# A two-block transformer kernel: the mLSTM recurrence on 64-row tiles with its maxima spread by transfers, and attention's preparation and masks moved inside the retention chunks

## The chip, the cores and the metric

One program on one core of a Trainium2 chip. The metric is the device time of one execution in microseconds (us), from the first to the last instruction and what the launch adds around it. Data are float32 throughout. The engines are TensorE (PE, with PEld for its weight loads), VectorE (DVE), ScalarE (ACT), GpSimd (POOL) and SyncE (SP, which here only issues transfers). Each has its own in-order queue of instructions, and semaphores are the only order between them.

## The reference, cut to what matters

The program computes a first block (modulation, four token mixers, a SwiGLU) on a 1024 x 1024 activation with a context of 256 tokens, and then a second block (retention and a sparse attention side by side, an output projection, a gated embedding). Two places are changed. The first is the recurrence of the mLSTM mixer, 4 heads of 64, run in both directions over the tokens:

```
b = cumsum(fc);  logw = where(lower, b[t] - b[s] + ic[s], -inf);  inter = b + m
m_t = max(inter, max(logw));  w_inter = exp(inter - m_t)
s = (qc @ kc.T) * exp(logw - m_t)
num = s @ vc + w_inter * (C @ qc);  den = sum(s) + w_inter * (n @ qc)
h = num / max(abs(den), exp(-m_t))
C = decay * C + e * vc x kc;  n = decay * n + e * kc
```

The second is the pair of retention (8 heads of 64) and sparse attention (8 heads, keys and values from a latent of width 128, each query keeps its 256 best keys):

```
scores = (qc @ kc.T) * intra;  o_intra = scores @ vc;  o_cross = (qc * xi) @ state
state  = chunk_decay * state + (kc * zeta).T @ vc
ret    = head_group_norm(o_intra + o_cross, ret_norm) * silu(r_g)

score  = sum_h wi * relu(qi @ k_idx.T);  top_val, top_idx = top_k(score, 256)
logits = (q_nope @ w_uk) . c_kv[top_idx] + q_pe . k_pe[top_idx]
out    = softmax(logits) @ c_kv[top_idx] @ w_uv
```

## The kernel before

Ten stages follow one another, and each is a block: all engines leave one before they enter the next. Tokens are tiled by P = 128, so the 1024 tokens are NT = 8 tiles and the context NCT = 2. Every stage has one program for each engine, and the order inside an engine's program is the order of its queue.

**stage_mixers** computes the mixers' projections, the short convolution and the gates, and ends with the mLSTM recurrence: 20 steps, 10 tiles in each of 2 directions taken in turn. The first 4 steps (the context) only update the state, the other 16 give output, and the code numbers those `lat` 0 to 15. A direction has four PSUM banks, `4 * d` to `4 * d + 3`. In an output step

- POOL copies the queries into a block-diagonal `qp` (L983), scales the keys into `ke` (L969), and adds the finished output into `H` (L996);
- PE makes the scores of two heads at a time against `qp` (L1109), the products with the carried state `CF` (L1113), the spread of the running maxima over the partitions as products with a selector `sel` (L1096), the state's update (L1126) and the values (L1133);
- DVE adds the keys' column and the mask into `arg` (L1363), ACT takes its exponential (L1203), DVE multiplies it with the scores into `PT` (L1373), scales the carried product into `num` (L1381), updates the state `CS` (L1387), adds the values (L1392), and divides by the bounded denominator (L1395 to L1399).

After the last step the output is normalised by head (L1408 to L1418), transposed, and the next stage starts.

**stage_retention** walks the 8 tiles in order. In tile i, PE makes the scores (L2477) against a block-diagonal `qpad`, transposes the queries and keys of tile i + 1 and attention's queries of it (L2467), makes the update of the state (L2486) from keys that POOL has scaled into `rkz` (L2549), and the output (L2499, L2501) from the state, the weighted scores and a padded copy of the values `vpad`. ACT evicts the transposes (L2512 to L2521) and the output (L2535). DVE multiplies the scores with the decay table (L2591), decays and updates the state (L2596, L2602) and normalises the output of tile i - 1 (`norm`, L2572 to L2580). POOL's order in tile i is: `rkz` (L2549), `xq` (L2554), the gate with the norm's weight (L2555), and the gated product of tile i - 1 (L2559), which waits for that tile's `norm`.

**stage_attention** first prepares: PE transposes the latent (L2671, L2672) and the matrix `uk` (L2675), and makes the values (L2683, 8 products of 512 columns) and the keys (L2691, L2692, 16 products). DVE makes the masks of the tiles 7, 6, 5 and 4 (`mask`, three parts: a count of what lies over the threshold and the flags of what equals it, L2859 to L2861; a running sum of the flags, L2863; the choice, L2865 and L2866), and ACT turns each into 0 or -1e30 (L2788). Then 64 steps (8 tiles of 8 heads, tile 7 first) make logits (L2705), softmax, transposes (L2717) and output (L2730).

**stage_first_end** loads the narrow slab of the second block's input weights in 8 pieces of 2 transfers, each with a semaphore of its own (L1919 to L1921), and splits them on ACT (L1993).

Of the kernel before, what the change touches and what calls it, by code (L numbers as in the profile page):

```python
# [24 lines left out]
P = 128  # L25
# [788 lines left out]
def stage_mixers(K):  # L814
# [38 lines left out]
    mask = K.at("mx_mask", 190.75, [P, 2, P])  # L853
    sel = [K.at(f"mx_sel{d}", kb, [P, HEADS, P]) for d, kb in enumerate((191.75, 6))]

    qp = [K.at(f"mx_qp{d}", 2 + 2 * d, [P, HEADS, P]) for d in range(2)]
# [6 lines left out]
    def columns(n):  # L863
# [22 lines left out]
             "g1 g2 g3 gx gmm ga gb colmm colev st argmm argr pr ptr smm qmm pvmm nr ker umm hr yam yae eps1 eps2 chain pchain").split()  # L886
# [10 lines left out]
    with nc.Block() as block:  # L897
        @block.sync
        def _(sp):
# [18 lines left out]
            load(3)  # L918
            sp.wait_ge(S["pvmm"], 2 * NT)
# [5 lines left out]
        def _(pool):  # L925
# [7 lines left out]
            for t in (selp, mask, *sel, CF, *qp, pair_rows[0]):  # L933
                link(g.memset(t[:], 0.0))
            link(g.memset(d0[:], 1.0))
            for r in (0, 32):
                link(g.affine_select(out=selp[r:r + 4], in_=selp[r:r + 4], compare_op=ALU.not_equal, fill=1.0, base=0,
                                     pattern=[[-2, 2], [-1, 2], [0, HD]], channel_multiplier=1))
                s = sel[r // 32][r:r + 4]
                link(g.affine_select(out=s, in_=s, compare_op=ALU.not_equal, fill=-1.0, base=0,  # L940
                                     pattern=[[-1, HEADS], [0, P]], channel_multiplier=1))
# [3 lines left out]
            link(g.affine_select(out=mask[:, 0, :], in_=mask[:, 0, :], compare_op=ALU.is_ge, fill=LOW, base=0,  # L945
                                 pattern=[[1, P]], channel_multiplier=-1))
            link(g.affine_select(out=mask[:, 1, :], in_=mask[:, 1, :], compare_op=ALU.is_ge, fill=LOW, base=0,
                                 pattern=[[-1, P]], channel_multiplier=1))
# [24 lines left out]
            def queries(n):  # L973
                step, d = steps[n]
                lat = n - 2 * NCT
                if lat < 0:
                    return
                if lat >= 2:
                    pool.wait_ge(S["qmm"], lat - 1)
                tok = slice((order[d][step] - NCT) * P, (order[d][step] - NCT + 1) * P)  # L980
                for a in range(2):
                    hr = slice(a * HD, (a + 1) * HD)
                    g.tensor_copy(qp[d][hr, a::2, :], qkT[hr, 0:2, tok]).then_inc(S["qp"], 1)  # L983
                pool.wait_ge(S["qp"], 2 * (lat + 1))
# [3 lines left out]
            for n, (step, d) in enumerate(steps):  # L988
                lat = n - 2 * NCT
                if n + 2 < len(steps):  # L990
                    queries(n + 2)
                    keys(n + 2)
                if lat >= 0:
                    c = order[d][step] - NCT
                    pool.wait_ge(S["xr"], lat + 1)
                    g.tensor_tensor(H[:, c], H[:, c], num[d][:, :, 0:HD], ALU.add).then_inc(S["hadd"], 1)  # L996
                    pool.wait_ge(S["hadd"], lat + 1)

        @block.tensor
        def _(pe):  # L1000
# [88 lines left out]
            def argument(n):  # L1089
                step, d = steps[n]  # L1090
                c = order[d][step]
                if c < NCT:
                    return
                pe.wait_ge(S["st"], n - 1)
                for h in range(HEADS):
                    last = nc.tensor.matmul(K.bank[4 * d][:, h * P:(h + 1) * P], sel[d][:, h, :], lrows[:, c * P:(c + 1) * P], start=True, stop=True)  # L1096
                last.then_inc(S["argmm"], 1)

            for n, (step, d) in enumerate(steps):
                c, lat = order[d][step], n - 2 * NCT  # L1100
                b = [K.bank[4 * d + m] for m in range(4)]
                tok = slice((c - NCT) * P, (c - NCT + 1) * P)
                if lat >= 0:
                    if lat >= 2:
                        pe.wait_ge(S["nr"], lat - 1)
                    pe.wait_ge(S["st"], n - 1)
                    pe.wait_ge(S["qp"], 2 * (lat + 1))
                    for j in range(2):
                        last = nc.tensor.matmul(b[1].rearrange("p (h t) -> p h t", h=HEADS)[:, 2 * j:2 * j + 2, :], qkT[:, 2 + j, tok],  # L1109
                                                qp[d][:, 2 * j:2 * j + 2, :], start=True, stop=True)  # L1110
                    last.then_inc(S["smm"], 1)
                    for h in range(HEADS):
                        last = nc.tensor.matmul(b[2][:, h * P:(h + 1) * P], qp[d][:, h, :], CF[:, d, h // 2 * HX:h // 2 * HX + P],  # L1113
                                                start=True, stop=True)
                    last.then_inc(S["qmm"], 1)
                if n + 1 < len(steps):
                    argument(n + 1)
                if step < NL - 1:
                    pe.wait_ge(S["ker"], n + 1)
                    if lat >= 0:  # L1120
                        pe.wait_ge(S["argr"], lat + 1)
                    elif n >= 2:
                        pe.wait_ge(S["st"], n - 1)
                    for h in range(HEADS):
                        o = (h // 2) * HX
                        last = nc.tensor.matmul(b[0][(h % 2) * HD:(h % 2 + 1) * HD, o:o + HX], ke[d][:, h, :], vx[:, c, h, :],  # L1126
                                                start=True, stop=True)
                    last.then_inc(S["umm"], 1)
                if lat >= 0:
                    pe.wait_ge(S["ptr"], lat + 1)  # L1130
                    for h in range(HEADS):
                        o = (c * HEADS + h) * HX
                        last = nc.tensor.matmul(b[3][:, h * P:(h + 1) * P], PT[d][:, h, :], vflat[:, o:o + P], start=True, stop=True)  # L1133
                    last.then_inc(S["pvmm"], 1)
# [8 lines left out]
        def _(act):  # L1143
# [54 lines left out]
            for q in range(4):  # L1198
                act.wait_ge(S["yb_tr"], q + 1)
                nc.scalar.activation(K.yT[2 + q // 2][:, (q % 2) * HALF:(q % 2 + 1) * HALF], K.bank[q][:], ACT.Copy).then_inc(S["yb_ev"], 1)  # L1200
            for m in range(2 * NT):
                act.wait_ge(S["argr"], m + 1)
                nc.scalar.activation(arg[m % 2][:], arg[m % 2][:], ACT.Exp).then_inc(S["pr"], 1)  # L1203
# [18 lines left out]
        def _(dve):  # L1222
# [118 lines left out]
            link(v.tensor_tensor(chunked(lf), chunked(lf), before, ALU.max))  # L1341
            link(v.tensor_tensor(chunked(win), before, chunked(lf), ALU.subtract))
# [13 lines left out]
            def argument(n):  # L1356
                step, d = steps[n]
                c = order[d][step]
                if c < NCT:
                    return  # L1360
                dve.wait_ge(S["argmm"], n - 2 * NCT + 1)
                for h in range(HEADS):
                    last = v.scalar_tensor_tensor(out=arg[d][:, h, :], in0=K.bank[4 * d][:, h * P:(h + 1) * P], scalar=COL[:, 1, c, 1, d, h:h + 1],  # L1363
                                                  in1=mask[:, d, :], op0=ALU.add, op1=ALU.min)
                last.then_inc(S["argr"], 1)

            for n, (step, d) in enumerate(steps):
                c, lat = order[d][step], n - 2 * NCT
                b = [K.bank[4 * d + m] for m in range(4)]
                if lat >= 0:  # L1370
                    dve.wait_ge(S["pr"], lat + 1)
                    dve.wait_ge(S["smm"], lat + 1)
                    v.scalar_tensor_tensor(out=PT[d][:], in0=b[1].rearrange("p (h t) -> p h t", h=HEADS), scalar=HD ** -0.5, in1=arg[d][:],  # L1373
                                           op0=ALU.mult, op1=ALU.mult).then_inc(S["ptr"], 1)
                if n + 1 < len(steps):
                    argument(n + 1)
                if lat >= 0:
                    if lat >= 2:
                        dve.wait_ge(S["hadd"], lat - 1)
                    dve.wait_ge(S["qmm"], lat + 1)  # L1380
                    link(v.tensor_tensor(num[d][:], b[2].rearrange("p (h e) -> p h e", h=HEADS)[:, :, 0:HX],  # L1381
                                         COL[:, 0, c, 0, d, :].unsqueeze(2).to_broadcast([P, HEADS, HX]), ALU.mult))
                if step < NL - 1:
                    dve.wait_ge(S["umm"], n + 1)
                    for j in range(2):
                        o = j * HX
                        last = v.scalar_tensor_tensor(out=CS[:, d, j, :], in0=CS[:, d, j, :], scalar=dcol[:, d, j, c:c + 1],  # L1387
                                                      in1=b[0][:, o:o + HX], op0=ALU.mult, op1=ALU.add)
                    last.then_inc(S["st"], 1)
                if lat >= 0:  # L1390
# [1746 lines left out]
```

## Time and profile before

| | |
|---|---|
| time, median of 3 runs | 2272.81 us (2270.8 to 2273.53) |
| the profiled execution: its time, its span | 2270.93 us, 2269.1 us |
| PE busy in the span | 2117.0 us (93%) |
| DVE busy | 1278.9 us (56%) |
| ACT busy | 733.0 us (32%) |
| POOL busy | 435.1 us (19%) |
| mean granted TensorE clock | 0.963 |

A row of a timeline gives the start and the duration in us from the start of the span, the engine, the line of the kernel, the operation, what it writes and reads, the number of instructions merged into the row, and in brackets the engine's idle time ahead of it and what ended that. The busy share of an engine is an average over stages with different limits, so what a change in one stage is worth is read in that stage. A float32 product is two MATMUL instructions, a transpose one.

### The profile page before, as it was taken

The page shows a single profiled execution, that of the slowest core. Times are in us where ns is not written, and L with a number is a line of the kernel's source. Part 1 is how long each engine was busy: PE and PEld are TensorE (multiplying, and loading weights), DVE is VectorE, ACT ScalarE, POOL GpSimd, SP SyncE. Part 2 cuts the span into 40 slices and gives each one's busy share as a digit, 9 for nine tenths or more (in the row PEclk, how much of TensorE's full clock was granted, in tenths as well). Part 3 has the DMA queues.
Part 4 walks back from the last instruction along what each step waited for, and adds up shares of the span by engine and source line. Part 5 has one row for each costly group of instructions (what it writes and reads, how often), then busy time and mean ns, then how long its engine had stood idle before and what let it go on. Part 6 is the DMA issues. An engine that isn't in the chain of part 4 may idle for free. (4 is left out here: it accounts for less than half of the span.)

```text
span 2269.1 us, 27732 instructions
## 1 busy us (share of the span) xinstructions
PE 2117.0 (93%) x10549; PEld 1599.9 (71%) x10549; DVE 1278.9 (56%) x2211; ACT 733.0 (32%) x1292; POOL 435.1 (19%) x501
## 2 busy tenths in 40 slices
PE   7998999995969999999999998889999868989998
PEld 4744464484858888888888886856888764658876
DVE  6591895278864333223454324478999577762433
ACT  2222021122113323223444223356121335761415
POOL 2900011042310000000000001223666440300210
PEclk8999999997989999999999999899999889999999
DMA  8543110003233333334434232122211002003101
GB/s 325 155 134 116 42 46 1 0 2 121 75 102 93 93 97 89 90 106 147 121 111 130 81 97 87 58 56 61 66 47 50 20 3 81 2 25 130 51 0 75
DMA packets 187512, 180.59 MB, mean 80 GB/s; under 512 B 12982, under 2 KB 157686, under 8 KB 184074
## 3 DMA queue, kind: packets, MB, share of 16 engines
q1 hardware_dynamic: 184426, 168.61, 23.9%
q0 software_dynamic: 2880, 10.49, 1.2%
q8 instruction: 70, 1.15, 0.2%
q14 instruction: 40, 0.33, 0.0%
q10 hardware_dynamic: 96, 0.02, 0.0%
HBM read 165.18 MB, written 12.60 MB: 78 GB/s over the span
## 5 line engine op out<-in xcount | busy, mean ns | idle before, releaser
L1800 DVE TENSOR_TENSOR ff_part<-ff_raw,ff_part 128x1024 fp32r<-128x1024 f32 (+2 forms) x152 | 164.9, 1085 | 435.5 <-ACT ff_part L1708 435.5
L1708 ACT ACTIVATE ff_part<-ff_raw 128x1024 fp32r<-128x1024 f32 (+2 forms) x152 | 144.0, 948 | 433.4 <-PE ps L1598 430.9
L1596 PE MATMUL ps<-h,ff_part 128*128 128x512 f32 x704 | 275.5, 391 | 4.7 <-DVE ff_part L1800 4.7
L1598 PE MATMUL ps<-h,ff_part 128*128 128x512 f32 x704 | 274.7, 390 | 0.0
L1597 PE MATMUL ps<-h,ff_part 128*128 128x512 f32 x704 | 274.7, 390 | 0.0
L2416 DVE TENSOR_SCALAR_CACHE_REDUCE pj_junk<-NM,prm 128x384 uint8<-128x384 f32 (+1 forms) x186 | 163.7, 942 | 1.1
L1596 PEld LDWEIGHTS ps<-h,ff_part 128*128 128x128 f32 x704 | 132.8, 189 | 32.3 <-DVE ff_part L1800 5.1
L1596 PE MATMUL ps<-pj_part,h 128*128 128x512 f32 x384 | 153.2, 399 | 0.2 <-ACT PJ L2273 0.2
L1597 PEld LDWEIGHTS ps<-h,ff_part 128*128 128x128 f32 x704 | 132.8, 189 | 27.4
L1598 PEld LDWEIGHTS ps<-h,ff_part 128*128 128x128 f32 x704 | 132.6, 188 | 27.6
L1597 PE MATMUL ps<-pj_part,h 128*128 128x512 f32 x384 | 150.4, 392 | 0.0
L1598 PE MATMUL ps<-pj_part,h 128*128 128x512 f32 x384 | 150.2, 391 | 0.0
L1597 PE MATMUL ps<-ff_hid,ff_part 128*128 128x512 f32 x352 | 137.0, 389 | 0.0
L1598 PE MATMUL ps<-ff_hid,ff_part 128*128 128x512 f32 x352 | 137.0, 389 | 0.0
L1596 PE MATMUL ps<-ff_hid,ff_part 128*128 128x512 f32 x352 | 137.0, 389 | 0.0
L2358 POOL TENSOR_TENSOR pj_part<-pj_raw,pj_part 128x512 fp32r<-128x512 f32 x64 | 84.7, 1326 | 160.3 <-ACT pj_part L2268 159.0
L1596 PE MATMUL ps<-w_end,se_hT 128*128 128x512 f32 x256 | 106.9, 418 | 0.4 <-DVE se_hT L3066 0.4
L1003 PE MATMUL ps<-mx_w,HT 128*128 128x272 f32 (+1 forms) x320 | 106.2, 493 | 0.0
L1598 PE MATMUL ps<-w_end,se_hT 128*128 128x512 f32 x256 | 100.0, 390 | 0.0
L1597 PE MATMUL ps<-w_end,se_hT 128*128 128x512 f32 x256 | 99.7, 390 | 0.0
L1596 PEld LDWEIGHTS ps<-pj_part,h 128*128 128x128 f32 x384 | 72.5, 189 | 29.4 <-issue 14.4
L1003 PEld LDWEIGHTS ps<-mx_w,HT 128*128 128x128 f32 x320 | 60.7, 190 | 44.2 <-issue 38.0
(601 smaller groups left out, 4057.7 us busy)
## 6 DMA issues: line engine op xcount, KB each, us to landing
ff_raw<-in_w_ffn_in SPq DMA_DIRECT2D x88, 512.0 KB, 3.7
s_wm<-in_w_mod SPq DMA_DIRECT2D x16, 1024.0 KB, 4.9
pj_raw<-in_w_in SPq DMA_DIRECT2D x64, 256.0 KB, 2.7
ff_raw<-in_w_ffn_out SPq DMA_DIRECT2D x32, 384.0 KB, 3.4
ff_raw<-in_w_ffn_out SPq DMA_DIRECT2D x32, 320.0 KB, 3.0
mod_w<-in_w_mod SPq DMA_DIRECT2D x8, 1024.0 KB, 8.9
mod_x<-in_x SPq DMA_DIRECT2D x8, 512.0 KB, 13.9
w_out<-in_w_out SPq DMA_DIRECT2D x4, 1024.0 KB, 8.7
```

What stands on the lines that cost most here:

```text
L1003: mm = nc.tensor.matmul(bank[:, 0:cols], lhs, rhs, start=(k == 0), stop=(k == KT - 1))
L1596: nc.tensor.matmul(out, w[0], x[0], start=first, stop=False)
L1597: nc.tensor.matmul(out, w[0], x[1], start=False, stop=False)
L1598: return nc.tensor.matmul(out, w[1], x[0], start=False, stop=last)
L1708: nc.scalar.activation(part[s % 2][0][:, 0:n, :], raw[s][:, 0:n, :], ACT.Copy).then_inc(hi, 1)
L1800: v.tensor_tensor(part[s % 2][1][:, 0:n, :], raw[s][:, 0:n, :], part[s % 2][0][:, 0:n, :].bitcast(F32), ALU.subtract).then_inc(lo, 1)
L2358: g.tensor_tensor(part[k % NR][1][:], raw[k % NR][:], part[k % NR][0][:].bitcast(F32), ALU.subtract).then_inc(S["lo"], 1)
L2416: last = v.tensor_scalar(junk[:, packed(j + 2)], x, bound(j), 0.0, ALU.is_ge, ALU.add, accum_out=cnt[:, j:j + 1])
```

## The change

Mixers, recurrence:

- The block-diagonal `qp` and POOL's two copies for it go. Scores and carried products read `qkT` directly, a head's 64 rows at a time, even heads into one bank and odd heads into another (`place` gives the order of heads in `arg` and `PT`).
- The products with `sel` go, and so do `sel`, `mask` and their preparation. Once DVE has the running maxima, they are written to DRAM, and SP reads them back for each step into a ring of 8 tiles `spread` of 128 x 512, each row repeated over all partitions (16 transfers of 256 KB in pieces of 512 bytes). POOL hides the future with an affine select on the tile (`hide`), 4 steps ahead.
- ACT takes the exponential straight from the ring, a head at a time with the keys' column as bias (`weights`), and scales the carried product (`carried`), also a head at a time. DVE's `argument` and the first product into `num` go, and its closing work of a step is done a step later (`finish`). POOL's addition into `H` is a step later too.
- The values' product takes 65 columns in place of 128.

Retention and attention:

- `qpad`, `vpad` and ACT's copies for them go: scores and output work on 64 rows or 64 columns a head. The scaled keys are written over the keys. The state's decay is done by ACT, a head pair at a time. Attention's queries are transposed ahead of the chunks.
- The transposes of the latent, attention's keys and values, the matrix `uk` and its transfers leave stage_attention. The latent is transposed at the start of the retention and evicted by DVE; in each chunk PE makes one tile of the values and one half row of the keys in bank 2, and ACT evicts both.
- The mask of tile 7 is made by DVE ahead of the chunks, one part of the masks 6, 5 and 4 in each chunk after `norm`, the last one at the end; ACT lowers them in chunks 1, 4 and 7 and at the end.
- SP loads the tables `intra` and `xi` and the norm's row only after attention's queries have been transposed.

First end: the 8 pieces of the narrow slab share 4 semaphores.

The core of the diff:

```diff
+            sp.wait_ge(S["lfr"], 1)
+            for d in range(2):
+                sp.dma_start(lf_dram[d], lf[32 * d:32 * d + HEADS, :]).then_inc(lf_out, 16)
+            sp.wait_ge(lf_out, 32)
+            sp.wait_ge(S["mm"], total)
+            for m in range(2 * NT):
+                step, d = steps[2 * NCT + m]
+                c = order[d][step]
+                if m >= RING:
+                    sp.wait_ge(S["pr"], m - RING + 1)
+                sp.dma_start(spread[m % RING][:], lf_dram[d:d + 1, :, c * P:(c + 1) * P].to_broadcast([P, HEADS, P])).then_inc(lf_in[m % RING], 16)
...
             for n, (step, d) in enumerate(steps):
                 lat = n - 2 * NCT
                 if n + 2 < len(steps):
-                    queries(n + 2)
                     keys(n + 2)
+                if n == 0:
+                    for m in range(4):
+                        hide(m)
                 if lat >= 0:
-                    c = order[d][step] - NCT
-                    pool.wait_ge(S["xr"], lat + 1)
-                    g.tensor_tensor(H[:, c], H[:, c], num[d][:, :, 0:HD], ALU.add).then_inc(S["hadd"], 1)
+                    hide(lat + 4)
+                if lat >= 1:
+                    gather(lat - 1)
...
+                for j in range(2):
+                    for a in range(2):
+                        r = slice(HD * a, HD * (a + 1))
+                        nc.tensor.matmul(b[a][:, j * P:(j + 1) * P], qkT[r, 2 + j, tok], qkT[r, j, tok], start=True, stop=True)
+                for j in range(2):
+                    for a in range(2):
+                        r = slice(HD * a, HD * (a + 1))
+                        last = nc.tensor.matmul(b[a][:, 2 * P + j * HX:2 * P + (j + 1) * HX], qkT[r, j, tok], CS[r, d, j, :], start=True, stop=True)
...
+            for n in range(len(steps)):
+                update(n)
                 if n + 1 < len(steps):
-                    argument(n + 1)
+                    scores(n + 1)
+                values(n)
...
+                for h in range(HEADS):
+                    last = nc.scalar.activation(arg[d][:, place(h), :], spread[m % RING][:, h, :], ACT.Exp, scale=-1.0, bias=COL[:, 1, c, 1, d, h:h + 1])
+                for h in range(HEADS):
+                    o = 2 * P + h // 2 * HX
+                    last = nc.scalar.activation(num[d][:, h, :], K.bank[4 * d + 1 + h % 2][:, o:o + HX], ACT.Copy, scale=COL[:, 0, c, 0, d, h:h + 1])
...
+            for i in range(NT):
+                turn_queries(i)
+                turn_latent(i)
...
+                prepare(2 * i)
+                if i + 1 < NT:
                     pe.wait_ge(S["kzr"], i + 1)
...
+                prepare(2 * i + 1)
                 pe.wait_ge(S["prob"], i + 1)
...
+            for part in range(3):
+                mask(FIRST[0], part)
             dve.wait_ge(S["const"], 80)
...
                 if i + 1 < NT:
                     new = state[1 - s]
                     if i:
-                        link(v.tensor_tensor(new[:], state[s][:], decay.unsqueeze(2).to_broadcast([P, J, P]), ALU.mult))
+                        dve.wait_ge(S["dec"], i)
                     dve.wait_ge(S["upd"], i + 1)
...
                 if i:
                     norm(i - 1)
+                mask(FIRST[1 + i // 3], i % 3)
             norm(NT - 1)
+            mask(FIRST[3], 2)
```

## Rows read from the trace of the kernel before

**Rows 1.** Windows by engine: length, then busy us (instructions) of PE, PEld, DVE, ACT, POOL; clock.

```profile
464.40:531.20 66.80, 63.48 (x548) 58.77 (x546) 59.15 (x201) 9.45 (x15) 29.24 (x56) 1.00 0.03 6
...
1782.70:1867.70 85.00, 61.90 (x400) 56.71 (x400) 53.34 (x100) 33.91 (x73) 43.71 (x37) 0.86 0.04 13
1867.70:1899.90 32.20, 27.60 (x68) 13.78 (x68) 23.96 (x30) 13.41 (x34) 0.66 (x2) 0.85 0.41 145
```

**Rows 2.** Timeline of one output step of the recurrence.

```profile
489.83 1.06 PE L1096 MATMUL ps<-mx_lf,mx_sel 128*128 128x128 f32 x8
...
490.32 0.68 POOL L996 TENSOR_TENSOR mx_H<-mx_H,mx_num 128x256 f32<-128x256 f32 x1 [1.84 <-DVE mx_num L1399]
...
490.81 0.45 PE L1126 MATMUL ps<-mx_vx,mx_ke 128*64 128x65 f32 x8
490.92 1.12 DVE L1363 SCALAR_TENSOR_TENSOR mx_arg<-ps,mx_COL,mx_mask 128x128 f32<-128x128 f32 x4
...
491.19 1.16 PE L1133 MATMUL ps<-mx_vx,mx_PT 128*128 128x128 f32 x8
...
491.99 0.61 POOL L969 TENSOR_TENSOR mx_ke<-mx_kn,mx_COL 128x256 f32<-128x256 f32 x1
...
492.41 0.47 DVE L1387 SCALAR_TENSOR_TENSOR mx_CS<-mx_CS,prm,ps 128x65 f32<-128x65 f32 x2
492.81 0.42 DVE L1392 TENSOR_TENSOR mx_num<-mx_num,ps 128x260 f32<-128x260 f32 x1
...
493.95 1.06 PE L1096 MATMUL ps<-mx_lf,mx_sel 128*128 128x128 f32 x8
494.22 0.68 DVE L1373 SCALAR_TENSOR_TENSOR mx_PT<-ps,mx_arg 128x512 f32<-128x512 f32 x1
```

**Rows 3.** Timeline of retention's start: POOL's keys alone, the first weighted scores.

```profile
1791.86 1.04 POOL L2549 TENSOR_TENSOR rt_kz<-PJ,prm 128x512 f32<-128x512 f32 x1
...
1792.48 1.29 DVE L2591 TENSOR_TENSOR rt_prob<-ps,rt_intra 128x512 f32<-128x512 f32 x2 [14.76 <-PE ps L2477]
```

**Rows 4.** Timeline of retention: one round of POOL, PE and DVE.

```profile
1815.94 1.29 POOL L2559 TENSOR_TENSOR PJ<-PJ 128x512 f32<-128x512 f32 x1 [4.88 <-DVE PJ L2580]
...
1824.70 0.69 DVE L2580 TENSOR_TENSOR PJ<-PJ,prm 128x512 f32<-128x512 f32 x1
...
1826.77 1.49 POOL L2549 TENSOR_TENSOR rt_kz<-PJ,prm 128x512 f32<-128x512 f32 x1
...
1829.58 0.85 DVE L2602 TENSOR_TENSOR rt_state<-rt_state,ps 64x256 f32<-64x256 f32 x2 [2.22 <-PE ps L2486]
```

**Rows 5.** Timeline of attention's logits, 64-row tiles: start of eight and of what follows.

```profile
1911.70 1.99 PE L2705 MATMUL ps<-at_kT,dqT 64*128 64x512 f32 x8
1913.61 1.09 PE L2717 MATMUL ps<-ident,at_prob 128*128 128x128 f32 x8
```

**Rows 6.** Groups of ACT: the eviction of 128 x 128.

```profile
L2761 ACT ACTIVATE at_latT<-ps 128x128 f32<-128x128 f32 x8 | 2.3, 283 | 3.4 <-PE ps L2672 3.4
```

**Rows 7.** One line of POOL: an affine select over 512 columns.

```profile
L940 POOL TENSOR_SCALAR_AFFINE_SELECT mx_sel<-mx_sel x2: 625/626/626, 329.9 to 331.3; 4x512 f32<-4x512 f32 x2
```

**Rows 8.** Transfers by tile: KB, median us from issue to landing.

```profile
at_wuv<-in_w_uv SPq DMA_DIRECT2D x1, 256.0 KB, 2.9
```

**Rows 9.** Timeline of retention's last chunk: POOL and DVE at once.

```profile
1856.16 1.27 POOL L2555 TENSOR_TENSOR PJ<-PJ,rt_row 128x512 f32<-128x512 f32 x1
1856.26 1.71 DVE L2574 TENSOR_TENSOR PJ<-PJ,prm 128x512 f32<-128x512 f32 x1
```

**Rows 10.** Timeline of attention's preparation: DVE's masks of the tiles 7 and 6.

```profile
1868.14 1.26 DVE L2859 TENSOR_SCALAR_CACHE_REDUCE at_flag<-NM,prm 128x1024 uint8<-128x1024 f32 x1
...
1875.39 1.15 DVE L2859 TENSOR_SCALAR_CACHE_REDUCE at_flag<-NM,prm 128x896 uint8<-128x896 f32 x1
...
1877.49 2.02 DVE L2863 TENSOR_TENSOR_SCAN at_run<-at_flag 128x896 f32<-128x896 uint8 x1
...
1881.92 1.01 DVE L2859 TENSOR_SCALAR_CACHE_REDUCE at_flag<-NM,prm 128x768 uint8<-128x768 f32 x1
```

More of the change, by code:

```diff
@@ L932, in _ @@
             link = Link(g, S["pchain"])
[L933 removed]
+            for t in (selp, CF, pair_rows[0]):
                 link(g.memset(t[:], 0.0))
@@ L1087, in _, with scores @@
             pe.wait_ge(S["yb_ev"], 4)
[L1089 removed]
+            def scores(n):
                 step, d = steps[n]
[L1091 to L1092 removed]
+                c, lat = order[d][step], n - 2 * NCT
+                if lat < 0:
                     return
[L1094 to L1097 removed]
@@ new lines, in values @@
+            def values(n):
+                step, d = steps[n]
+                c, lat = order[d][step], n - 2 * NCT
+                if lat < 0:
+                    return
+                pe.wait_ge(S["ptr"], lat + 1)
+                if lat >= 2:
+                    pe.wait_ge(S["nr"], lat - 1)
+                for h in range(HEADS):
+                    last = nc.tensor.matmul(K.bank[4 * d + 3][:, h * P:h * P + HX], PT[d][:, place(h), :], vx[:, c, h, :], start=True, stop=True)
+                last.then_inc(S["pvmm"], 1)
@@ L2445, in stage_retention @@
     mu, var = (K.prm[:, 16 + RH * n:16 + RH * (n + 1)] for n in range(2))
-    names = "zero vr const tr qkr dqr smm prob xqr kzr out oev upd state var gate norm done chain".split()
+    K.kfT = K.at("at_kT", 24, [P, J, T])
+    K.val = K.at("at_v", 40, [P, NT, AH * AD])
+    lat_pe = K.at("at_latpe", 80, [P, 2, T])
+    latT, peT = lat_pe[:, 0], lat_pe[:, 1]
+    ukT = K.at("at_ukT", SMALL_KB, [P, J, P])
+    wuv = K.at("at_wuv", SMALL_KB + 2, [P, AH, AD])
+    spread = K.at("at_spread", SMALL_KB + 4, [P, 2, AD])
+    uk = K.wsT
+    names = ("zero const tr qkr dqt dqr smm prob xqr kzr out oev upd state var gate norm done chain "
+             "clear uk wuv spread dec turn latr ukr pre prer pick masked").split()
     S = {n: K.sem("rt_" + n) for n in names}
@@ L2531, in _ @@
                     take(i + 1)
+                prepared(2 * i)
+                if 0 < i < NT - 1:
+                    act.wait_ge(S["state"], i)
+                    for j in range(J):
+                        last = nc.scalar.activation(state[1 - i % 2][:, j, :], state[i % 2][:, j, :], ACT.Copy, scale=decay[:, j:j + 1])
+                    last.then_inc(S["dec"], 1)
+                prepared(2 * i + 1)
                 if i:
```

435 lines of the change are left out of this document (217 added, 218 removed).

## The prediction

> **What bounds the kernel now.** I read the page's slices first, then the windows of the stages that the diff touches, then the timeline inside one period of each, since both are loops. Three stretches matter [rows 1]. In the recurrence's output part PE (63.5 of 66.8 us) and DVE (59.2) are both nearly full. In the retention (85.0 us) no engine is: PE 61.9, DVE 53.3, POOL 43.7, ACT 33.9. Attention's preparation takes 32.2 us, with PE busy for 27.6, and POOL does almost nothing there.
>
> One step of the recurrence repeats every 4.12 us, from L1096 to the next L1096 [rows 2]. PE issues 36 instructions in it without a pause: eight of L1096 take 0.98 us to issue (0.12 each), eight of L1126 with 65 columns 0.38 (0.048), L1133 goes like L1096. The reader is to see that DVE's programme is as long: it goes from the argument at 490.92 to the next PT at 494.22 with gaps of some 0.03 only.
>
> In the retention a ring of waits sets the pace, not an engine. POOL's L2559 starts at 1815.94 and the next of its kind about 9.6 us later: `norm` ends at 1825.39 (1824.70 + 0.69), POOL multiplies by the gate (1.29), scales the keys (1.49, from 1826.77), PE makes the update (1.2), DVE adds it to the state at 1829.58, and then comes the next `norm`, which ends about 5.4 later [rows 4]. So from the end of `norm` to the state's addition pass 4.19 us, in which DVE has only the scores and the decay to do.
>
> The preparation is a sequence ahead of the first logits and ends where PE's products end.
>
> **The recurrence, part by part.** DVE: the argument and the carried product go, which is 490.92 to 492.41, 1.49 us. Left are 4.12 - 1.49 = 2.63 us [rows 2]. PE: L1096's 0.98 goes. The scores become eight instructions of 128 columns on alternating halves of the rows. The nearest rows are attention's logits, already in such halves: eight of 512 columns in 1.91 us, 0.24 each [rows 5], about half of four times 0.12. So I take 0.06 each, 0.5 us; the upper end is 0.12, 1.0 us. Carried product, update and values are eight instructions of 65 columns each: 0.38 us by L1126, up to 1.0 by L1133, if 128 columns of weights set the pace. PE needs 1.7 to 3.4 us (0.5 to 1.0, 0.4, and twice 0.4 to 1.0); I take 2.4. ACT: eight pieces of at most 0.28 [rows 6], 2.3 us instead of 0.63. POOL: the copies go, an affine select of 0.63 comes [rows 7]; with 0.68 for H and 0.61 for the keys [rows 2] and gaps it has 2.2 us. The transfers: the nearest is 256 KB in pieces of half the size, which landed after 2.9 us [rows 8]; eight are under way ahead of use, so 2.9 a step would still be hidden. The cover gone, a step would be as long as a transfer.
>
> No engine alone needs more than 2.6. But POOL and DVE get in each other's way: in the last chunk DVE's product takes 1.71 us behind a POOL product that ends 1.2 us after it began, where the same kind takes 0.69 [rows 9, 4]. In the new step POOL's three operations run from DVE's last product on, 2.25 us. DVE meanwhile does PT, the states and the first addition (0.68 + 0.40 + 0.45 = 1.55, with PSUM as an input), then comes to the small products and the scaling, 494.22 - 493.26 = 0.96 us (the addition at 492.81 takes 0.45 with its gap) [rows 2], all from SBUF. If those must wait for POOL's third operation, the step is 2.25 + 0.96 = 3.2. With a little for handshakes I take 3.25. Bounds: 2.63 without exclusion; 3.6 if PE needs its upper end with changes of tile shape between.
>
> Between the first and last PT lie 15 steps: 15 x (4.12 - 3.25) = 13.0 us gained. At the head POOL makes four selects (2.6 us) between the keys of steps 2 and 3; the context's updates wait, but the first PT waited for the argument before. I charge 0.5. The first ring tiles are read once the last slab's products are done, some 6 us before use, so they are hidden. The tail has the same chain. Recurrence: -12.5 us (bounds -22 and -7). Everything behind it moves up.
>
> **Retention and preparation.** Gone: 32.2 us of preparation [rows 1]. Added, at three places:
>
> Front. Before, the first weighted scores came at 1792.48 [rows 3], 9.8 us into the stage. Now 60 transposes at 0.12 us, the first 13 or so at twice that (8 to 9 us), and DVE's eight evictions stand first, until about 1791. Then comes the mask of tile 7, 7.25 us (1868.14 to 1875.39) [rows 10], and POOL's first two products (1.04 [rows 3] and 1.3, released by the late tables near 1795.5) fall between its parts. First weighted scores near 1800.6, +8.1; about +7.5 is left at the first `norm`'s end, as chunk 0 was waiting for other things too.
>
> Chunks. Each gets a mask part between `norm` and the scores. For tile 6 these are 2.10, 2.06 and 2.37 us (1875.39 to 1877.49; the scan with its gap; the rest up to 1881.92) [rows 10]; the scores take 1.29 [rows 3]. By length alone, at most 2.37 + 1.29 = 3.7 fits into the 4.19, and the ring would stay near 9.3 (the decay has left DVE, and POOL's keys, 1.49 beside it [rows 4], take 1.04 alone [rows 3]). But the part's operations start 0.1 us ahead of POOL's gated product. With exclusion: count part, the flags wait for the keys, state at 4.6; scan 2.0 + 1.29 + 1.04 + 1.2 = 5.6; choice, two passes with a POOL product between them, 5.8. Over 4.19 that is 0.4, 1.4 and 1.6. No row shows a scan beside POOL; it has two inputs from SBUF like the row that waited [rows 9], so I take the full wait, and nothing as the lower end. Five rounds carry a part (scan, choice, count, scan, choice, the last three shorter): +6.1 us.
>
> The Trainium skill (SBUF — State Buffer, "SBUF: two separate sides") has it that VectorE with two SBUF inputs and a GpSimd operation share one port pair under an exclusive lock, and the loser blocks for the whole instruction. The product that waited agrees (1.71 for 0.69) [rows 9]; for scan and choice no row here shows it. By that rule the chunks cost the 6.1 above, without it they would gain about 1.
>
> PE has some 7.8 us a chunk now (scores 1.0, transposes 1.0, three products of 512 columns and two passes 2.6, update 1.0, output 2.2), below the ring. ACT has 4.1 us and in three chunks 0.9 more. Their place in the queue matters: the second product of the preparation stands between update and output, 1.7 us, which the output can bear as long as it is evicted before the `norm` of the next round.
>
> Tail. The last mask's three parts (tile 4, some 5.0 us by columns, from 6.5 for tile 6) fall into the last two chunks and behind, with 0.7 for ACT to lower it; I guess that 1.3 of it hides in the wait for the last output. +4.4.
>
> Sum: 7.5 + 6.1 + 4.4 = 18.0 us added, 32.2 gone: -14.2. Without exclusion front and chunks lose 2.4 and 7.0 of that: -23. If PE or ACT hold up `norm` in each round by 1.3 us, -7. The first end's paired semaphores: a piece waits for the second pair's transfers, issued 0.9 us later, while PE has transposes to do; nothing.
>
> **Sum.** 2270.9 (the profiled execution) - 12.5 - 14.2 = 2244.2. The median of the runs, 2272.8, is 1.9 above that execution, so on its scale 2246.
>
> **Rivals.**
> - Exclusion costs little, since the queues fall into step so that POOL and DVE rarely meet, as they now do in the recurrence. For it: POOL is idle for half of both loops. Against: the new order starts both at the same event. Step 2.63, ring 9.3: -22 - 23 = -45, 2228.
> - Chunks and steps are longer: PE without the pairing's gain (step 3.6) and a queue in the chunks that holds `norm` up: -7 - 7 = -14, 2259.
> - The spreading by transfers doesn't do what it should: a read of 512-byte pieces takes a whole old step (4.1 us) once eight are queued. The recurrence gains nothing, 2259. Against it stands 2.9 [rows 8].
> - Slower than before: the clock. Granted were 0.86 in the retention with PE busy 73% of the time, 1.00 in the recurrence at 95% [rows 1]. Afterwards PE is busy for about 74% in both (2.4 of 3.25, 7.8 of 10.7). If it is granted the lower level throughout (1.2 GHz), a step takes 4.8 us (+10), and eight chunks of 15.6 and a front of 15 make 140 us against 117 now (+23): 2306. It decides from a mean near 0.6 in both on, below which a step (2.4 / 0.6 = 4.0) and a chunk (13) are as long as what they save. The 0.86 at the same share of busy time speaks against it.
>
> **Chances.** Forecast 0.56, exclusion costs little 0.18, longer steps and chunks 0.16, transfers 0.05, clock 0.05. The first has its own range of 2236 to 2257 (the uncertain sizes in step and ring). To leave out no more than 2 in 10 it must reach the neighbours on both sides, 2230 to 2262. Under 0.2% (4.5 us) this kernel can't tell a change. All but the clock are far on the fast side; a milder clock gives about 0.03 for no change: faster 0.92, same 0.03, slower 0.05.
>
> **What the next profile would show.** Right: PTs 3.2 to 3.3 us apart, DVE's first small product starting as POOL's third operation ends; the retention 103 us long, with rounds near 11.0, and DVE's scans followed at once by POOL's gated product; first logits about 0.4 us into attention. Wrong: PTs 2.6 apart or rounds near 9.3 with the scan beside a POOL product; ACT or PE busy up to each `norm`; a recurrence whose wait is for `spread`; a granted clock under 0.7.

## The result, and the profile after

The changed kernel takes 2258.25 us (median of 4 runs, 2257.96 to 2262.19) against 2272.96 for the kernel before: ratio 0.9945, 95% interval 0.9933 to 0.9958. That is 14.7 us faster, where 26.8 were forecast. The profiled execution takes 2257.96 us, its span is 2256.2 against 2269.1, and its mean granted clock 0.951 against 0.963.

Put side by side by stretches, the two executions differ so (us; "readout" is the first reduction of the recurrence's output; a norm counts to its last product's end):

| stretch | before | after | change | forecast |
|---|---|---|---|---|
| start to first PT | 464.45 | 464.85 | +0.4 | +0.5 |
| first to last PT | 62.35 | 63.96 | +1.6 | -13.0 |
| last PT to readout | 4.36 | 5.88 | +1.5 | 0 |
| readout to the retention's first instruction | 1251.54 | 1247.72 | -3.8 | 0 |
| to the first norm's end | 23.04 | 32.90 | +9.9 | +7.5 |
| first to sixth norm's end | 47.83 | 52.59 | +4.8 | +6.1 |
| sixth norm's end to the first logits | 46.38 | 17.49 | -28.9 | -27.8 |
| first logits to the second end | 136.81 | 138.74 | +1.9 | 0 |
| second end to the last instruction | 232.34 | 232.07 | -0.3 | 0 |

The retention with the preparation in it has shrunk by 14.3 us (14.2 forecast) and is 103.0 us long, as the prediction has it. The recurrence has gained nothing. The windows of the changed kernel, of the recurrence, the retention and attention's start, are (columns as in [rows 1]):

```profile
475.00:525.00 50.00, 50.00 (x365) 45.98 (x364) 30.12 (x93) 23.20 (x89) 19.43 (x30) 0.50 0.08 22
1782.40:1885.30 102.90, 77.96 (x532) 61.27 (x532) 79.69 (x132) 39.90 (x86) 48.83 (x35) 0.90 0.05 16
1885.30:1899.30 14.00, 10.39 (x32) 4.88 (x32) 5.82 (x12) 5.49 (x8) 0.00 (x0) 0.56 0.82 301
```

The first line is the surprise. PE is busy for all of the 50 us, and DVE, which was full before [rows 1], for 60% only; the granted clock is 0.50, which is the lower level (1.2 GHz), where it was 1.00. One step of the timeline shows the same from inside:

```profile
491.25 0.70 PE L1132 MATMUL ps<-mx_vx,mx_ke 128*64 128x65 f32 x8
491.88 1.23 PE L1116 MATMUL ps<-mx_qkT 64*128 64x128 f32 x8
492.00 0.48 DVE L1429 SCALAR_TENSOR_TENSOR mx_CS<-mx_CS,prm,ps 128x65 f32<-128x65 f32 x2 [1.63 <-PE ps L1132]
492.69 0.98 PEld L1120 LDWEIGHTS ps<-mx_CS,mx_qkT 64*128 64x128 f32 x8
492.90 0.96 PE L1120 MATMUL ps<-mx_CS,mx_qkT 64*128 64x65 f32 x8
493.78 1.78 PEld L1145 LDWEIGHTS ps<-mx_vx,mx_PT 128*128 128x128 f32 x8
493.79 1.97 PE L1145 MATMUL ps<-mx_vx,mx_PT 128*128 128x65 f32 x8
494.12 0.68 DVE L1421 SCALAR_TENSOR_TENSOR mx_PT<-ps,mx_arg 128x512 f32<-128x512 f32 x1
495.68 0.70 PE L1132 MATMUL ps<-mx_vx,mx_ke 128*64 128x65 f32 x8
```

A step is 4.43 us, from L1132 to L1132, and PE issues through all of it: 0.63, 1.02, 0.89 and 1.89 us for the four groups. The update's eight took 0.45 us before [rows 2], here 0.70; DVE waits 1.63 us for them. The last group, the values, is paced by its weight loads: eight of 128 columns in 1.78 us for products of only 65 columns.

When did the level fall? In both kernels ahead of the first output step. The context's updates of the kernel before, and what follows them:

```profile
459.17 0.45 PE L1126 MATMUL ps<-mx_vx,mx_ke 128*64 128x65 f32 x8 [0.58 <-POOL mx_ke L969]
461.62 0.70 PE L1126 MATMUL ps<-mx_vx,mx_ke 128*64 128x65 f32 x8
466.08 0.45 PE L1126 MATMUL ps<-mx_vx,mx_ke 128*64 128x65 f32 x8
```

and of the kernel after:

```profile
459.00 0.45 PE L1132 MATMUL ps<-mx_vx,mx_ke 128*64 128x65 f32 x8 [0.58 <-POOL mx_ke L977]
462.12 0.70 PE L1132 MATMUL ps<-mx_vx,mx_ke 128*64 128x65 f32 x8 [2.67 <-POOL mx_ke L977]
```

The same eight products tell the level: 0.45 us is the upper one, 0.70 the lower. Before, it was back at 466.08. After, it never came back in the recurrence: from 462.12 to 532.29, where the values' last group ends, PE is busy for 70.17 of 70.17 us and every duration is that of the lower level. The clock column shows that level for 99.0 us in a row, as PE's pauses behind the recurrence (11.3 and 6.4 us) are in it too; it follows the durations by some 10 us, so a short window can show the wrong one.

In the retention the rows of DVE and POOL that the prediction spoke of look as it said:

```profile
1799.92 1.29 DVE L2744 TENSOR_TENSOR rt_prob<-ps,rt_intra 128x512 f32<-128x512 f32 x2
...
1815.23 2.02 DVE L2474 TENSOR_TENSOR_SCAN rt_run<-rt_flag 128x896 f32<-128x896 uint8 x1
...
1815.47 2.85 POOL L2698 TENSOR_TENSOR PJ<-PJ 128x512 f32<-128x512 f32 x1 [9.39 <-DVE PJ L2720]
...
1827.06 2.04 POOL L2698 TENSOR_TENSOR PJ<-PJ 128x512 f32<-128x512 f32 x1 [5.28 <-DVE PJ L2720]
...
1829.08 1.88 POOL L2689 TENSOR_TENSOR PJ<-PJ,prm 128x512 f32<-128x512 f32 x1
...
1885.39 3.79 PE L2815 MATMUL ps<-at_kT,dqT 64*128 64x512 f32 x8 [11.16 <-PEq L2516]
...
1891.83 3.79 PE L2815 MATMUL ps<-at_kT,dqT 64*128 64x512 f32 x8 [2.65 <-DVE prm L2913]
...
1899.43 1.99 PE L2815 MATMUL ps<-at_kT,dqT 64*128 64x512 f32 x8
```

The gated product takes 1.29 us alone [rows 4]; beside the scan it takes 2.85 and ends 1.07 us after it, and beside the choice (1826.83 on) 2.04, with the keys behind it 1.88 in place of 1.04 [rows 3]. The last three rows show attention's start: its first logits now follow a pause of PE of 11 us, and two groups of eight take 3.79 us each where 1.99 is usual [rows 5]. Only the first of the two is new: in the kernel before the first group took 1.99 us (1899.95), but the second already 3.61 (1904.83).

### The profile page after: what moved, and what is told of

It reads as the page before. It is cut to its first block and busy times, and to the rows that moved or that the text cites. A ratio compares the mean times of both kernels' runs of the same rounds, so it can differ in the third digit from the quotient of the medians.

```text
span 2256.2 us, 27762 instructions
## 1 busy us (share of the span) xinstructions
PE 2104.8 (93%) x10549; PEld 1589.7 (70%) x10549; DVE 1262.5 (56%) x2133; ACT 746.2 (33%) x1380; POOL 432.4 (19%) x472
```

## The experiments

All are built on the changed kernel. Ratios are to the kernel before on the same chip, with 95% intervals. Experiments 1 to 4, 5 to 8 and 9 to 11 ran on three different chips (the kernel before took 2271.60, 2270.70 and 2271.06 us there), so between these groups the ratios are compared rather than the times.

**1. The mixers of before.** The function stage_mixers is that of the kernel before, the rest is the changed kernel.

> The mixers stage of the kernel before in the changed kernel, so only the retention and attention part of the change is left. Theory A (the recurrence gives nothing back since its products run at the lower clock; the retention part alone carries the gain): the last PT comes about 2 us earlier than in the changed kernel, but the stages behind absorb most of that, so 2256 to 2259 us, ratio 0.993 to 0.9945. Theory B (the recurrence does gain, and a loss elsewhere hides it): 2265 to 2270 us.

2258.92 us, ratio 0.9950 (0.9936 to 0.9963), the same as the whole change. In its trace the recurrence runs at a granted clock of 1.00, and its last PT comes 1.1 us earlier than in the changed kernel, not 2. So the retention's part carries all of the gain, and the mixers' part gives nothing (theory A).

**2. Wide values.**

```diff
-nc.tensor.matmul(K.bank[4 * d + 3][:, h * P:h * P + HX], PT[d][:, place(h), :], vx[:, c, h, :], ...)
+nc.tensor.matmul(K.bank[4 * d + 3][:, h * P:(h + 1) * P], PT[d][:, place(h), :], vflat[:, o:o + P], ...)
```

> The changed kernel with the values' product on 128 columns again in place of 65; eight more half products of 63 columns a step. The weight loads of 128 columns set its pace at either clock, so this costs nothing. Theory C (the clock follows the columns that are streamed; with 65 columns PE mostly loads weights): the level rises again a few us into the recurrence as it did before, the step falls from 4.43 to 3.2 us with the exclusion of my prediction (2.6 to 2.9 without), and the time to 2240 us (2233 without exclusion). Theory D (tiles of 64 rows keep it low, whatever the columns): the step stays at 4.43 and the time at 2258 us.

2236.09 us, ratio 0.9840 (0.9826 to 0.9853): 22 us less than the changed kernel for eight wider instructions a step. PTs are 2.51 us apart from 477.80 on. The level does rise, as theory C has it; the step is shorter than I had for either exclusion.

**3. A warm head.**

```diff
+            def idle(count):
+                for _ in range(count):
+                    nc.tensor.matmul(K.bank[3][:, 0:P], K.ident[:], K.ident[:], start=True, stop=True)
             for n in range(len(steps)):
                 update(n)
+                if n < 4:
+                    idle((2, 3, 12, 0)[n])
```

> The changed kernel with 17 products of 128 x 128 more in the pauses of PE among the context's updates (2, 3 and 12 of them, into a bank that nothing reads yet), so that PE has no pause before the recurrence. Theory E (the pause at the head alone brings the lower clock, and the steps then keep whichever level they start with): full clock through the whole recurrence, steps of 3.2 us, 2240 us. Theory C or D (the steps' own work is too little for the full clock): the level falls some steps into the recurrence, 2255 to 2258 us.

2233.74 us, ratio 0.9831 (0.9818 to 0.9845). The window of its recurrence and one step:

```profile
472.90:503.00 30.10, 29.98 (x391) 27.29 (x387) 28.46 (x98) 24.63 (x95) 20.63 (x32) 1.00 0.18 49
```

```profile
489.61 0.17 DVE L1416 TENSOR_TENSOR prm<-prm,mx_COL 128x4 f32<-128x4 f32 x1
489.66 0.63 POOL L987 TENSOR_SCALAR_AFFINE_SELECT mx_spread<-mx_spread 128x512 f32<-128x512 f32 x1
...
489.79 0.45 PE L1132 MATMUL ps<-mx_vx,mx_ke 128*64 128x65 f32 x8
489.81 0.18 DVE L1417 RECIPROCAL prm<-prm 128x4 f32<-128x4 f32 x1
490.02 0.55 DVE L1419 TENSOR_TENSOR mx_num<-mx_num,prm 128x256 f32<-128x256 f32 x1
...
490.17 0.71 PE L1116 MATMUL ps<-mx_qkT 64*128 64x128 f32 x8
490.49 0.68 DVE L1427 SCALAR_TENSOR_TENSOR mx_PT<-ps,mx_arg 128x512 f32<-128x512 f32 x1
...
490.65 0.68 POOL L994 TENSOR_TENSOR mx_H<-mx_H,mx_num 128x256 f32<-128x256 f32 x1 [0.36 <-DVE mx_num L1419]
490.71 0.56 PE L1120 MATMUL ps<-mx_CS,mx_qkT 64*128 64x65 f32 x8
...
491.23 1.11 PE L1145 MATMUL ps<-mx_vx,mx_PT 128*128 128x65 f32 x8
491.41 0.61 POOL L977 TENSOR_TENSOR mx_ke<-mx_kn,mx_COL 128x256 f32<-128x256 f32 x1
...
492.17 0.63 POOL L987 TENSOR_SCALAR_AFFINE_SELECT mx_spread<-mx_spread 128x512 f32<-128x512 f32 x1
```

The very products that ran at the lower level for the whole recurrence run at the upper one for the whole recurrence, if they enter it there (theory E). A step is 2.51 us: PE 2.47 (0.38, 0.54, 0.52 and 1.03), DVE as much. POOL's three operations fill 2.2 us of the step (the first from 490.65 on, the third, the select, to 492.80), with gaps of 0.08 and 0.15 us between them. DVE's small product with two inputs from SBUF (489.61) starts in the second gap of the round before, ahead of the select at 489.66, and takes its usual 0.17.

**4. Both wide.** The carried product as well on 128 columns.

> The values' product and the carried product both on 128 columns (the latter still 64 rows). Theory C: full clock as with wide values alone, the same 3.2 us a step, 2240 us; if wide values alone are just short of what the clock asks for, this one has it and the other not. Theory D: 4.43 us a step, 2258 us, as the carried product too is bound by its weight loads.

2235.82 us, ratio 0.9844 (0.9831 to 0.9858), 2.51 us a step: nothing beyond experiment 2, except that the level rises one step sooner (the second and third PT are 3.29 us apart, in experiment 2 still 4.46). It rises within the second group of carried products (1.06 us for the first eight at 465.54, 0.92 here), before a values' product has run at all:

```profile
468.18 0.92 PE L1120 MATMUL ps<-mx_CS,mx_qkT 64*128 64x128 f32 x8
469.02 1.16 PE L1145 MATMUL ps<-mx_vx,mx_PT 128*128 128x128 f32 x8
```

So it is not the values' product as such that brings the level back, and tiles of 64 rows do not keep it down (against theory D).

**5. The masks behind.** On top of the warm head, all parts of the masks 6, 5 and 4 come after the last norm.

> The warm head, and the masks of tiles 6, 5 and 4 made behind the last norm in place of one part in each chunk; nothing is left out. It measures what the parts cost in the chunks. By the prediction's step (length and exclusion together 6.1 us over the rounds) the rounds, measured from one norm's end to the next, fall from a mean of 10.5 to 9.3 us; behind the chunks come 17.2 us of masks where now 4.2 stand, so 2233.7 - 6.1 + 13 = 2241 us. Rival (the parts hide in waits and the rounds are held by PE or ACT): rounds stay at 10.4, 2247 us.

2239.00 us, ratio 0.9862 (0.9846 to 0.9879). The starts of the last products of the first and of the sixth norm, with a warm head alone:

```profile
1790.44 0.69 DVE L2726 TENSOR_TENSOR PJ<-PJ,prm 128x512 f32<-128x512 f32 x1
...
1843.03 0.69 DVE L2726 TENSOR_TENSOR PJ<-PJ,prm 128x512 f32<-128x512 f32 x1
```

and with the masks behind:

```profile
1788.90 0.69 DVE L2723 TENSOR_TENSOR PJ<-PJ,prm 128x512 f32<-128x512 f32 x1
...
1817.17 1.27 POOL L2701 TENSOR_TENSOR PJ<-PJ 128x512 f32<-128x512 f32 x1 [4.38 <-DVE PJ L2723]
...
1834.66 0.69 DVE L2723 TENSOR_TENSOR PJ<-PJ,prm 128x512 f32<-128x512 f32 x1
```

Rounds are 10.52 us with the parts and 9.15 without, 6.8 us over five. By kind, against 9.15: count +0.3, scan +1.3, choice +1.6 and +1.3 (the first round, with a scan at the lower clock, +2.4). The gated product is back at 1.27.

**6. No hide.** On top of the warm head, POOL's affine select is left out, and only its semaphore is counted up.

> The warm head, and POOL's affine select (hide) left out, so that the weights are not masked: what of DVE's step is held up by POOL at full clock. Theory F (each engine waits only for what it overlaps with in SBUF: the scaling takes 0.55 where it takes 0.43 alone): step 2.51 to 2.40 us, 2232 us. The prediction's step (three operations of POOL in a row, DVE's small products behind them) would give 2.5 to 1.9 or less, 2225 us; if POOL does not matter at all, 2.51 and 2234 us.

2232.55 us, ratio 0.9832 (0.9816 to 0.9847). PTs are 2.46 apart, and the scaling takes 0.43:

```profile
490.02 0.43 DVE L1417 TENSOR_TENSOR mx_num<-mx_num,prm 128x256 f32<-128x256 f32 x1
```

Of the 0.12 that it gets back, 0.05 shows, as PE is as long (theory F; the 2.40 was a little short of PE's own programme).

**7. Keys ahead.** On top of the warm head, in POOL's program of the retention:

```diff
                 g.tensor_tensor(K.PJ[:, R_G, i, :], K.PJ[:, R_G, i, :], row[:], ALU.mult).then_inc(S["gate"], 1)
+                scale_keys(i + 1)
                 if i:
```

and the keys no longer stand at the head of tile i (but for tile 0).

> The warm head, and POOL scales the keys of tile i + 1 before the gated product of tile i - 1, so that the update no longer waits for norm. Theory G (the ring norm, gated product, keys, update, state sets the rounds, as the prediction has it): the rounds fall from 10.5 to about 9.2, which is DVE's own work in a round, 7 us less, 2227 us. Rival (PE's queue or ACT's decay is as late): rounds stay over 10, 2232 to 2234 us.

2226.81 us, ratio 0.9808 (0.9794 to 0.9822). Rounds have a mean of 9.57 (first and sixth norm's products at 1787.91 and 1835.75), 4.7 us less over five, not 6.6: the meetings only move. The keys (1822.53, 1.04) now hold up a product of norm that takes 0.69 alone:

```profile
1822.63 1.49 DVE L2726 TENSOR_TENSOR PJ<-PJ,prm 128x512 f32<-128x512 f32 x1
```

The ring did set the rounds (theory G). By the ratios the gain over the warm head is 5.2 us, about what the rounds give. The rest of the 7 us by medians is not in the retention: this execution reaches its first PT 2.5 us sooner on the same code.

**8. Products of no use in other pauses.** On top of the warm head, 46 and 26 of 128 x 128 ahead of the two halves of the normalised output, and 11 of 128 x 512 behind the last output of the retention.

> The warm head, and more products of no use in three other pauses: 46 and 26 of 128 x 128 while DVE normalises the recurrence's output, 11 of 128 x 512 behind the last output of the retention. Theory H (what follows a pause runs at the lower clock for some us and can be had at full clock): attention's first two groups of logits take 1.99 us in place of 3.79 each, the first products of the join 1.9 for eight in place of 3.5, about 6 us less, 2228 us. Rival (the pause between two stages, or the end of PE's queue, lowers the clock anyhow, or the products come too late and hold up their queue): 2233 to 2236 us.

2228.09 us, ratio 0.9811 (0.9798 to 0.9824). Half of it works:

```profile
527.58 6.39 PE L1547 MATMUL ps<-w_out_hi,jn_yh 128*128 128x512 f32 x16 [2.32 <-ACT jn_yh L1568]
...
1858.45 1.99 PE L2831 MATMUL ps<-at_kT,dqT 64*128 64x512 f32 x8 [1.67 <-PEq L2530]
1863.09 2.83 PE L2831 MATMUL ps<-at_kT,dqT 64*128 64x512 f32 x8 [2.65 <-DVE prm L2929]
```

The first logits run at the upper level and the second partly; attention is 2.8 us shorter (135.9 for 138.8 of experiment 3). The gain over the warm head is 4.5 us by the ratios. The join gains next to nothing: its first 16 products take 6.2 us as they took 6.0, as two pauses of 1.5 and 2.3 us still stand between the products of no use and them.

**9. POOL's order at the head.** The changed kernel with the four selects spread among the keys, no added product.

> The changed kernel with POOL's four first selects spread between the keys of the context (one behind each of two keys, two behind the next) in place of four in a row, and no other change: PE's pause ahead of the last context update shrinks from 2.7 to about 1 us, and the first PT comes some 1.8 us earlier. Theory E2 (only the pause at the head decides the level): full clock from the first output step, 2232 us. Rival (what is left of the pauses still lowers the clock, and the steps then stay there): steps of 4.43 us, 2256 us.

2259.05 us, ratio 0.9949 (0.9935 to 0.9963), no gain, the rival:

```profile
460.70 0.45 PE L1136 MATMUL ps<-mx_vx,mx_ke 128*64 128x65 f32 x8 [0.58 <-POOL mx_ke L977]
462.07 0.70 PE L1136 MATMUL ps<-mx_vx,mx_ke 128*64 128x65 f32 x8 [0.91 <-POOL mx_ke L977]
```

The pause ahead of the last context update is down from 2.67 us to 0.91, and the level still falls between these rows and stays down. The kernel before could have told: there too the level falls at the head, and PE's pauses ahead of it are only 1.22, 0.58 and 0.58 us.

**10. Wide values in four steps.** As experiment 2, for the output steps 0 to 3 only.

> The changed kernel with 128 columns in the values' product of the first four output steps alone, 65 in the other twelve. If a recurrence that has once come back to full clock stays there on narrow products: the level rises in the first steps as with wide values throughout, and all later steps take 2.51 us, 2236 us. If the wide products are needed throughout: the level falls again after them and the steps return to 4.43, 2250 us or more. If four steps are too few for the rise: 2258 us.

2234.89 us, ratio 0.9842 (0.9828 to 0.9855): all of the gain.

```profile
468.41 2.07 PE L1147 MATMUL ps<-mx_vx,mx_PT 128*128 128x128 f32 x8
470.41 0.70 PE L1132 MATMUL ps<-mx_vx,mx_ke 128*64 128x65 f32 x8
471.04 1.03 PE L1116 MATMUL ps<-mx_qkT 64*128 64x128 f32 x8
471.91 0.56 PE L1120 MATMUL ps<-mx_CS,mx_qkT 64*128 64x65 f32 x8
472.39 1.16 PE L1147 MATMUL ps<-mx_vx,mx_PT 128*128 128x128 f32 x8
473.48 0.45 PE L1132 MATMUL ps<-mx_vx,mx_ke 128*64 128x65 f32 x8
```

One wide group at the lower level is enough here, as in experiment 2: by the next step all durations are those of the upper one. After the fourth step the products are narrow again, and PTs stay 2.4 to 2.5 us apart to the end.

**11. All together.** Warm head, keys ahead and products of no use.

> The warm head, the keys scaled ahead and the products of no use in the other three pauses together. The gains of the last two over the warm head, 7 and 5.5 us, lie in different places and should add: 2221 us. Rival (the shorter rounds leave PE less full and the clock falls in the chunks, or the extra products hold up the queue): 2226 us.

2226.23 us (2224.03 to 2228.02), ratio 0.9804 (0.9791 to 0.9817), within the intervals of experiments 7 and 8: the rival's time, though not clearly by its mechanism. In its trace the retention has the short rounds (9.57), but the first two groups of logits take 3.31 and 2.46 us (3.59 and 3.39 in experiment 7, 1.99 and 2.83 in experiment 8), so that attention is 1.1 us shorter than in experiment 7, not 2.8. The products of no use behind the retention are the same as in experiment 8; why they do less here stays open.

## Why the prediction was right and wrong

**The bound of the recurrence, wrong.** The failed step is "15 x (4.12 - 3.25) = 13.0 us gained". Measured in its place is a loss of 1.6 us (15 steps of 4.26 on average, 4.43 once the level is down throughout), and 1.5 more in the tail, which I had at 0. It rested on PE needing 2.4 us a step. At full clock that is right (2.47 in experiment 3), but the steps ran at 1.2 GHz, where PE needs 4.43 and is the bound. The slower rival had this very mechanism, at 4.8 us a step, and I gave it 0.05, for two reasons that don't hold. I tied both loops together, but the retention kept its clock (0.90). And I took the 0.86 of the retention at a like busy share as evidence, which says nothing of a loop that is entered at the lower level and is made of short products behind full weight loads. The level had already fallen at 461.62 in the kernel before, just ahead of the first window of [rows 1], and a search for what brought it back there would have led to the removed work: L1096 and L1113 stream 128 columns for 128 of weights, L1109 256.

The measured 2258 lies inside 2230 to 2262 and next to the 2259 of two of my rivals, but that is luck. The transfers never held the recurrence (`spread` landed after 3.4 us at the median, and PE never paused), and a step of 3.6 us with a longer queue in the chunks was not seen either.

What is shown: the clock alone costs the missing time. Experiments 2, 3 and 10 add only products or columns whose results are not read, and gain 22 to 25 us. Narrow products hold the upper level once they have it, to the end of the recurrence (3, 10), and never regained it from the lower in 70 us (after, 9). Wider values (2, 10) or wider carried products (4) at the lower level bring it back. The Trainium skill (TensorE: Matmul & The Clock Gate, "Part 1: The HAM clock gate") says that activity of the engine releases the clock. The window at 475 to 525 disagrees as far as busy time goes: PE was busy for 50.00 of 50.00 us and stayed at the lower level. The measurement decides: a PE that the profile shows as busy is no sign that the level will come back.

What is not shown is which property of the widened products counts, their columns or the time between weight loads. Nor is it shown which of the pauses at the head brings the level down: only filling all of them but the first was tried with success (3), shortening the longest was not enough (9).

**Exclusion in the recurrence, wrong too.** Exclusion is here that an operation of POOL or DVE stands still until the other's has ended. "If those must wait for POOL's third operation, the step is ... 3.2": at full clock it is 2.51, and leaving `hide` out saves 0.05 (experiment 6). That POOL's three operations take 2.25 us from DVE's last product on was right (490.57 to 492.80 in experiment 3). That DVE's products wait for the third was not: the one with two inputs from SBUF starts in the gap ahead of the select, and only the scaling is held, 0.12 us. This is a matter of where the products fall. In the changed kernel as written the small product starts inside the select and ends as it does, 0.48 us for 0.17:

```profile
492.87 0.64 POOL L987 TENSOR_SCALAR_AFFINE_SELECT mx_spread<-mx_spread 128x512 f32<-128x512 f32 x1
493.05 0.48 DVE L1410 TENSOR_TENSOR prm<-prm,mx_COL 128x4 f32<-128x4 f32 x1
```

There it costs nothing, as PE is the bound. My rival "exclusion costs little" had nearly the right step (2.63), had the clock been up. This error hid behind the first: with both right the forecast for the recurrence would have been some -24 us.

**Exclusion in the chunks, right.** Forecast +0.4, +1.4 and +1.6 for count, scan and choice; measured +0.3, +1.3 and +1.3 to 1.6. The five rounds cost 4.8 more than before for 6.1: the parts cost 6.8 (experiment 5), but the ring without them is 9.15, not 9.3, and 9.57 before. (Two sums in the prediction are off by a little: 0.68 + 0.40 + 0.45 is 1.53, and the scan's 2.0 + 1.29 + 1.04 + 1.2 is 5.53. Neither moves the forecast.) The reading of the ring held as well (experiment 7), though its rounds are 10.5 us where I looked for 11.0.

**Front, too small.** +9.9 for +7.5. The first weighted scores came +7.7 later in the stage (forecast +8.1). I let 0.6 of that be absorbed; instead 2.1 more were added up to the norm's end. The keys' update there waits 3.02 us for POOL and runs at the lower clock (L2598, 2.07 us for eight at 1798.86, 1.16 at 1831.01); no run separates the two.

**Tail, right.** -28.9 for -27.8. First logits are 0.06 us into attention, and ACT lowers the last mask at its door. That the three parts come to -14.3 us for -14.2 is in part luck: the front was 2.4 us too small, and chunks and tail 1.3 and 1.1 us too large.

**What was costed at nothing.** Attention's start is 1.9 us longer, again the clock: what used to stand ahead of it were PE's own products, now it is a pause. Between the readout and the retention 3.8 us came back. 1.8 of it in the join, whose second half waits for DVE in any case. The other 2.0 lies in the stages between join and retention, 1211.13 us before and 1209.10 after. The eleven experiments take 1209.62 to 1211.04 for the same stretch, so most of it may be no more than what executions differ by; whether the paired semaphores of the first end have a part in it was not tried.

**The sum.** The changed kernel with a warm head is 37.9 us faster than before, 23 more than as it was written. That is also 11.1 more than was forecast, which is the step of 2.51 us in place of 3.25, fifteen times.

## What to carry to other kernels

Before taking products away from a loop of PE, find the level it is entered at, by the duration of the same small group just ahead of it, and ask what in the loop brings it back up; a loop that has lost its wide products may hold the upper level and still never regain it. Columns that are added behind weight loads of the same width cost next to nothing on a path bound by those loads (1.16 us for 1.11, experiments 10 and 3) and were worth 1% of this kernel. And where two engines hold each other up, follow the meetings operation by operation: in the chunks one scan made a product of POOL 1.56 us longer, in the recurrence the same small product of DVE lost 0.31 us or nothing, by where it fell.

## What was not expected of the hardware

The same stream of products ran at 1.2 GHz for 70 us with PE never idle, and at 2.4 GHz for a whole recurrence with PE as busy (29.98 of 30.10 us), depending on the level at its entry alone. A single group of eight instructions on 128 columns in place of 65 ended the lower level. 17 products of no use, 34 instructions of some 0.12 us in PE's pauses, are worth 24 us. The clock column of the profile shows a change some 10 us after the durations do.
